# Dividing the last contraction, norm and stores at token 384 instead of 256

## The chip, the cores and the metric

One core of a Trainium2 chip. The metric is device microseconds of one execution. Engines are named as in the profile: PE is TensorE (matrix products; PEld its weight loads), DVE is VectorE, ACT is ScalarE, SP is SyncE, which issues nearly all DMAs. The program is written engine by engine, with semaphores between the engines; no scheduler moves anything.

## The reference

Two transformer blocks, 512 tokens, 1024 channels, float32. The change touches the end of the second one only: the down projection of its last MLP, the residual add, the final norm and the output.

```python
def rmsnorm(x, g):
    xf = x.astype(jnp.float32)
    y = xf * lax.rsqrt(jnp.mean(xf * xf, axis=-1, keepdims=True) + EPS) * g.astype(jnp.float32)
    return y.astype(x.dtype)

def sq_relu_mlp(h, w_up, w_down):
    u = jax.nn.relu(h @ w_up)
    return (u * u) @ w_down

def second_block(x, ..., ln_final):
...
        h = h + sq_relu_mlp(rmsnorm(h, ln_mlp[layer]), w_up[layer], w_down[layer])
    return rmsnorm(h, ln_final)
```

## The kernel before

Activations lie with channels on the 128 partitions and tokens along a row: `h` is 8 chunks of 128 channels by 512 tokens. A product with float32 accuracy is made of three (`exact3`): high weights by high data, low weights by high data, high weights by low data, where high and low are a rounded float32 kind (fp32r in the profile's rows) that TensorE takes in one pass. Each of the three loads its own 128 x 128 weights. A plain float32 product, as in the column sums, is one row of the program and two records in the trace.

The last MLP's down projection adds to `h` group by group. The very last of its work is kept apart, and is the stage that the change touches: output chunks 4 to 7 (`j` of 0 to 3), contracted over the last 8 groups of 128 hidden channels (`kt`), from the weight blocks `N_END - 2` and `N_END - 1`. So a chunk is 8 x 3 = 24 products. This stage is made in two parts of the tokens (`th` of 0 and 1), all four chunks for the first part, then all four for the second. Before, the parts are `HALF`: tokens 0 to 255 and 256 to 511.

For each part and chunk the work goes around the engines:

- PE, `last_chunk`: 24 products into one of two PSUM banks (X[2], X[3]); the third chunk waits for the residual add of the first to free its bank (`tl_h`), and so on.
- DVE, `last_resid`: adds the bank to `h` and ends in `tl_h`.
- ACT, `last_square`: squares the new chunk into a scratch tile.
- DVE, `last_add`: adds the squares to a running sum (the squares of chunks 0 to 3 are in it already).

After a part's four chunks comes its norm: PE's `last_norm` sums over partitions (a product with ones, plain float32), ACT's `last_rsqrt` makes rstd by Ln and Exp, DVE's `last_scale` multiplies each of the eight chunks of `h` by the weight and rstd, and SP stores each chunk when it is scaled (`h_final`), in the order of the chunks, one DMA of 128 rows each. The first part's norm is woven into the second part's products: in PE's order `last_norm(0)` stands behind the second part's first chunk, and in DVE's order `last_scale(0)`, all eight, stands behind the second part's first residual add. Each engine takes its instructions strictly in the order written.

Of the kernel before, what the change touches and what calls it, by code (L numbers as in the profile page):

```python
# [20 lines left out]
T = 512  # L21
# [209 lines left out]
def program(nc, A, out):  # L231
# [4 lines left out]
    with ctx:  # L236
# [205 lines left out]
        def wide(t):  # L442

            return t.rearrange("p k n -> p (k n)").rearrange("p (k n) -> p k n", k=4)
        HALF = (slice(0, T // 2), slice(T // 2, T))

        def copies(w):
            return w[:, :, 0:P].rearrange("p k (j n) -> p k j n", j=4)[:, :, :, 0:GLR]
# [879 lines left out]
        @block.sync  # L1328
        def _(sp):
            def raw_free(n):  # L1330

                if n >= 4 and n - 4 in FAST:
                    sp.wait_ge(S["st_mm"], 7 * FAST[n - 4] + PRODUCT_NO["P4"])
                elif n >= 4 and n - 4 in MLP_AT:
                    sp.wait_ge(S["acc_done"], DONE[n - 3])
                elif n >= 4:
                    sp.wait_ge(S["w_lo_ready"], STD_NO[n - 4] + 1)

            def load(n, src, cols=BW):

                raw_free(n)
                sp.dma_start(raw[:, n % 4, :, 0:cols], src).then_inc(w_arrived[n % 4], 16)

            def load_plain(first):
                _, count, w, col = next(x for x in plain if x[0] == first)
                cols = GLR if first == N_GLR else BW
                for j in range(count):
                    load(first + j, w[:, :, col + BW * j:col + BW * j + cols], cols)

            def load_wide_part(n, w, half, j):  # L1350
                raw_free(n + j)
                sp.dma_start(wide(raw[:, (n + j) % 4]),
                             w[:, 4 * half:4 * half + 4, 512 * j:512 * j + 512]).then_inc(w_arrived[(n + j) % 4], 16)

            def load_wide(n, w, half):
                for j in range(2):
                    load_wide_part(n, w, half, j)

            def load_mlp(n):
                up, down = mlps[n]  # L1360
                for i in range(32):
                    _, _, kind, g, b = MLP_AT[n + i]
                    if kind == "U":
                        load(n + i, up[:, :, 512 * g + BW * b:512 * g + BW * b + BW])
                    else:
                        raw_free(n + i)
                        sp.dma_start(wide(raw[:, (n + i) % 4]),
                                     down[:, 4 * g:4 * g + 4, 512 * b:512 * b + 512]).then_inc(w_arrived[(n + i) % 4], 16)

            _, _, first, col = next(x for x in plain if x[0] == N_DQ)  # L1370
            sp.dma_start(raw[:, 0, 0:4, :], first[:, 0:4, col:col + BW]).then_inc(S["ld_w0"], 16)
            sp.dma_start(vec[:], A["vecs"]).then_inc(S["ld_vec"], 16)
            for c in range(KT):
                if c == 2:
                    sp.dma_start(raw[:, 0, 4:8, :], first[:, 4:8, col:col + BW]).then_inc(w_arrived[0], 16)
                sp.dma_start(h[:, c, :], A["x"][:, c, :]).then_inc(S[f"ld_x{c}"], 16)
            load(N_DQ + 1, first[:, :, col + BW:col + 2 * BW])
            sp.dma_start(cst[:], A["consts"]).then_inc(S["ld_const"], 16)
            for n in (N_DK, N_DV, N_RW, N_RW + 1):
                load_plain(n)  # L1380
            for n in (N_MK, N_MV):
                load_plain(n)
            load_wide(N_WOA, mix_w, 1)
            sp.wait_ge(S["acc_done"], DONE[N_WOA])

            def reload(c):
                sp.dma_start(h[:, c, :], A["x"][:, c, :]).then_inc(S[f"ld_x{c}"], 16)

            for c in range(4):
                reload(c)  # L1390
            sp.wait_ge(S["acc_evac"], ACC[N_WOA] + 1)
            load_wide_part(N_WOB, mix_w, 0, 0)
            sp.wait_ge(S["acc_evac"], ACC[N_WOA] + 2)
            for c in range(4, KT):
                reload(c)
            sp.wait_ge(S["acc_evac"], ACC[N_WOA] + 4)
            load_wide_part(N_WOB, mix_w, 0, 1)
            sp.wait_ge(S["acc_evac"], ACC[N_WOA] + 5)
            load_plain(N_MQ)
            load_wide(N_MOA, mo_w, 0)  # L1400
            load_wide(N_MOB, mo_w, 1)
            load_mlp(N_MLP1)
            for n in (N_GLR, N_GQK, N_GV, N_GG, N_GOUT):
                load_plain(n)
            load_mlp(N_MLP2)
            for n in (N_KV, N_WQ):
                load_plain(n)
            load_wide(N_SOA, so_w, 0)
            load_wide(N_SOB, so_w, 1)
            load_mlp(N_MLP3)  # L1410
            for th in range(2):
                for c in range(KT):
                    sp.wait_ge(S["h_final"], KT * (th + 1) + c + 1)
                    sp.dma_start(out[:, c, HALF[th]], h[:, c, HALF[th]]).then_inc(S["st_out"], 16)
            sp.wait_ge(S["st_out"], 16 * 2 * KT)


# [75 lines left out]
        def _(pe):  # L1493
# [490 lines left out]
            def last_chunk(th, j):  # L1984
                c = j % 2
                if th == 0 and j == 0:
                    wait("st_ev", 2 * len(FAST))
                if 4 * th + j >= 2:
                    wait("tl_h", 4 * th + j - 1)
                ws = slice(j * P, j * P + P)  # L1990
                for kt in range(KT):
                    m = N_END - 2 + kt // 4
                    if th == 0 and j == 0 and kt % 4 == 0:
                        block_ready(m)
                    u_hi, u_lo = u_of(2, 12 + kt // 2)
                    last = exact3(X[2 + c][:, 0:T // 2], wide(hi_of(m))[:, kt % 4, ws], wide(lo_of(m))[:, kt % 4, ws],
                                  u_hi[:, kt % 2, HALF[th]], u_lo[:, kt % 2, HALF[th]], kt == 0, kt == KT - 1)
                last.then_inc(S["tl_done"], 1)

            def last_norm(th):  # L2000
                wait("tl_add", 4 * (th + 1))
                mm(X[th][:, 0:T // 2], C("ones"), nt[2][:, HALF[th]], start=True, stop=True).then_inc(S["tl_step"], 1)

            for th in range(2):
                for j in range(4):
# [7 lines left out]
        def _(act):  # L2013
# [352 lines left out]
            def last_square(th, j):  # L2366
                act.wait_ge(S["tl_h"], 4 * th + j + 1)
                if j < 2:
                    act.wait_ge(S["norm_add"], 7 * 7 + 3)
                else:  # L2370
                    act.wait_ge(S["tl_add"], 4 * th + j - 1)
                nc.scalar.activation(nt[j % 2][:, HALF[th]], h[:, 4 + j, HALF[th]], ACT.Square).then_inc(S["tl_sq"], 1)

            def last_rsqrt(th):
                act.wait_ge(S["tl_step"], 3 * th + 1)
                nc.scalar.activation(rstd[:, HALF[th]], X[th][:, 0:T // 2], ACT.Ln, scale=1.0 / D,
                                     bias=C("eps6")).then_inc(S["tl_step"], 1)
                act.wait_ge(S["tl_step"], 3 * th + 2)
                nc.scalar.activation(rstd[:, HALF[th]], rstd[:, HALF[th]], ACT.Exp, scale=-0.5).then_inc(S["tl_step"], 1)

            for th in range(2):
                for j in range(4):
# [7 lines left out]
        def _(dve):  # L2390
# [555 lines left out]

            def last_resid(th, j):
                dve.wait_ge(S["tl_done"], 4 * th + j + 1)
                h_ = h[:, 4 + j, HALF[th]]
                TTO(h_, h_, X[2 + j % 2][:, 0:T // 2], ALU.add).then_inc(S["tl_h"], 1)  # L2950

            def last_add(th, j):
                dve.wait_ge(S["tl_sq"], 4 * th + j + 1)
                if j:
                    dve.wait_ge(S["tl_add"], 4 * th + j)
                else:
                    dve.wait_ge(S["norm_add"], 7 * 7 + 3)
                TTO(nt[2][:, HALF[th]], nt[2][:, HALF[th]], nt[j % 2][:, HALF[th]], ALU.add).then_inc(S["tl_add"], 1)

            def last_scale(th):  # L2960
                dve.wait_ge(S["tl_step"], 3 * th + 3)
                for c in range(KT):
                    STT(h[:, c, HALF[th]], h[:, c, HALF[th]], V("ln_final_2", c), rstd[:, HALF[th]], ALU.mult,
                        ALU.mult).then_inc(S["h_final"], 1)

            for th in range(2):
                for j in range(4):
                    last_resid(th, j)
                    if j:
                        last_add(th, j - 1)  # L2970
                    elif th:
                        last_scale(0)
                last_add(th, 3)
            last_scale(1)


INPUTS = ["x", "mem", "norm_mix_w", "w_in", "mu_shift", "w_decay0", "w_decay_up", "a0", "a_up", "g_up", "k_k", "k_a", "r_k",
# [26 lines left out]
```

## Time and profile before

| | |
|---|---|
| time, median of 3 runs | 1936.69 us (1936.63 to 1937.65) |
| profiled execution, first to last instruction | 1937.4 us |
| mean granted TensorE clock | 0.998 |
| PE busy | 1912.2 us, 99% |
| DVE busy | 1333.0 us, 69% |
| ACT busy | 837.4 us, 43% |
| last stage's products, first to last | 1904.57 to 1928.20 us |
| after them, to the end of the span | 9.2 us |

The span is the time from the program's first to its last instruction in the one execution that was profiled; times in the trace are counted from its start. The page gives no other time for that execution. An instruction's record can be longer than the distance to the next of its kind, since both PE's products and its loads overlap: for a stream, the distance from start to start counts, and it is worked out from merged rows ("x8") as the row's length less one record, over the count less one.

### The profile page before, as it was taken

To read this page: it belongs to the slowest core of one execution; us is meant where nothing else is said; L and a number is where in the kernel's file an instruction comes from. 1 tells how busy PE (TensorE), PEld (TensorE's weight loads), DVE (VectorE), ACT (ScalarE), POOL (GpSimd) and SP (SyncE) were. 2 spreads that over 40 slices of the span, in tenths; PEclk is the share of its full clock that TensorE was granted. 3 is DMA by queue.
4 is the path that set the end of the run, shared out by engine and by line. 5 is a ranking of instruction groups with operands and counts; after the bars stand their busy time and mean duration, and the time that the engine had idled before them with its cause. 6 is when DMAs were issued, how large, how long until landed. Compare 5 with 4: busy or idle time off the path is not lost.

```text
span 1937.4 us, 32713 instructions
## 1 busy us (share of the span) xinstructions
PE 1912.2 (99%) x14002; PEld 1646.6 (85%) x14002; DVE 1333.0 (69%) x1755; ACT 837.4 (43%) x1254; POOL 121.1 (6%) x130
## 2 busy tenths in 40 slices
PE   8999999999999999999999999999999999999998
PEld 6877898888788898887989889889987788898897
DVE  5576869576677777767545687767677768777665
ACT  4333744344354344344224443434444645344342
POOL 1055100000000000010000000000002300000000
PEclk9999999999999999999999999999999999999999
DMA  8221402237123233224220233323342113233231
GB/s 271 88 66 66 137 10 80 88 132 128 46 89 108 87 110 109 88 78 140 90 87 23 66 98 98 109 87 109 102 144 88 50 47 106 90 106 109 87 109 44
DMA packets 138831, 182.62 MB, mean 94 GB/s; under 512 B 4917, under 2 KB 103429, under 8 KB 138304
## 3 DMA queue, kind: packets, MB, share of 16 engines
q1 hardware_dynamic: 135392, 168.91, 26.9%
q0 software_dynamic: 3296, 11.63, 2.9%
q8 instruction: 111, 1.82, 0.4%
q14 instruction: 32, 0.26, 0.0%
HBM read 172.66 MB, written 7.34 MB: 93 GB/s over the span
## 4 chain that ended last, share of the span: by engine, by line
PE 94%; DVE 3%; ACT 1%; issue 1%; DMA 0%; SPq 0%; DVEq 0%; ACTq 0%
PE X L1597 20%; PE M L1509 19%; PE M L1510 19%; PE M L1511 19%; PE X L643 3%; PE M L1570 1%; PE M L1571 1%; PE M L1572 1%; PE M L1925 1%; PE X L1902 1%; PE X L1913 1%; PE X L1780 1%; PE X L1749 1%; DMA raw<-in_w_in_dram 0%; PE X L1511 0%
## 5 line engine op out<-in xcount | busy, mean ns | idle before, releaser
L1510 PE MATMUL M<-u,raw_lo 128*128 128x512 f32 x728 | 287.9, 396 | 0.0
L1509 PE MATMUL M<-u,w_hi 128*128 128x512 f32 x728 | 287.9, 395 | 0.0
L1511 PE MATMUL M<-u,w_hi 128*128 128x512 f32 x728 | 286.1, 393 | 0.0
L2021 ACT ACTIVATE w_hi<-raw 128x2048 fp32r<-128x2048 f32 x113 | 215.6, 1908 | 93.5 <-PE M L1511 47.9
L2076 ACT ACTIVATE us<-X 128x256 f32<-128x256 f32 x156 | 60.2, 386 | 426.9 <-PE X L1597 426.9
L2549 DVE TENSOR_TENSOR h<-h,M 128x512 f32<-128x512 f32 x184 | 123.7, 685 | 144.7 <-PE M L1511 144.6
L1597 PE MATMUL X<-t,w_hi 128*128 128x256 f32 x936 | 173.2, 282 | 0.0
L1511 PEld LDWEIGHTS M<-u,w_hi 128*128 128x128 f32 x728 | 137.6, 189 | 32.8
L1509 PEld LDWEIGHTS M<-u,w_hi 128*128 128x128 f32 x728 | 136.8, 188 | 30.8
L1510 PEld LDWEIGHTS M<-u,raw_lo 128*128 128x128 f32 x728 | 136.7, 188 | 29.8
L2399 DVE TENSOR_TENSOR raw_lo<-raw,w_hi 128x2048 fp32r<-128x2048 f32 x57 | 130.3, 2287 | 23.7 <-ACT w_hi L2021 23.7
L1597 PEld LDWEIGHTS X<-t,w_hi 128*128 128x128 f32 x936 | 146.4, 188 | 0.0
L2399 DVE TENSOR_TENSOR w_lo<-raw,w_hi 128x2048 fp32r<-128x2048 f32 x52 | 118.9, 2289 | 29.9 <-ACT w_hi L2021 29.9
L1597 PE MATMUL X<-t,w_lo 128*128 128x256 f32 x468 | 131.7, 281 | 0.0
L1597 PE MATMUL X<-f,wx 128*128 128x256 f32 x624 | 117.8, 282 | 0.0
L1597 PEld LDWEIGHTS X<-f,wx 128*128 128x128 f32 x624 | 98.6, 189 | 1.7
L2480 DVE TENSOR_TENSOR w_lo<-w_sum,w_hi 128x1024 fp32r<-128x1024 f32 x78 | 91.9, 1220 | 0.0
L1597 PEld LDWEIGHTS X<-t,w_lo 128*128 128x128 f32 x468 | 88.2, 188 | 0.0
L1597 PE MATMUL X<-f,raw_lo 128*128 128x256 f32 x312 | 87.9, 282 | 0.0
L1509 PE MATMUL M<-gx_hi,w_hi 128*128 128x512 f32 (+2 forms) x232 | 85.1, 367 | 1.0 <-DVE w_lo L2399 0.5
L1511 PE MATMUL M<-gx_lo,w_hi 128*128 128x512 f32 (+2 forms) x232 | 84.3, 363 | 0.0
L1510 PE MATMUL M<-gx_hi,w_lo 128*128 128x512 f32 (+2 forms) x232 | 84.3, 363 | 0.0
(525 smaller groups left out, 4542.2 us busy)
## 6 DMA issues: line engine op xcount, KB each, us to landing
raw<-in_w_up_dram SPq DMA_DIRECT2D x48, 1024.0 KB, 5.4
raw<-in_w_down_dram SPq DMA_DIRECT2D x48, 1024.0 KB, 5.0
raw<-in_w_in_dram SPq DMA_DIRECT2D x12, 1024.0 KB, 8.6
raw<-in_a_w_in_dram SPq DMA_DIRECT2D x12, 1024.0 KB, 5.3
h<-in_x_dram SPq DMA_DIRECT2D x16, 256.0 KB, 4.8
raw<-in_w_mk_dram SPq DMA_DIRECT2D x4, 1024.0 KB, 4.9
raw<-in_w_mv_dram SPq DMA_DIRECT2D x4, 1024.0 KB, 5.2
raw<-in_w_out_dram SPq DMA_DIRECT2D x4, 1024.0 KB, 5.1
```

The source lines that it names most:

```text
L643: last = mm(blk(bank, hh, cp, cpar), a_, b_, start=True, stop=True)
L1509: mm(dst, wh, xh, start=start, stop=False)
L1510: mm(dst, wl, xh, start=False, stop=False)
L1511: return mm(dst, wh, xl, start=False, stop=stop)
L1570: mm(o_, hi[:, kt, ts_], w_hi[:, n % 2, kt, cs], start=kt == 0, stop=False)
L1571: mm(o_, hi[:, kt, ts_], w_lo[:, n % 2, kt, cs], start=False, stop=False)
L1597: last = mm(region(r), (wl if p_ == 1 else wh)[:, m, :], xl if p_ == 2 else xh, start=name in ("P1", "P2", "P4", "P5") and m == 0 and p_ = ...
L2021: nc.scalar.activation(hi_of(n)[:, :, :], raw[:, n % 4], ACT.Copy).then_inc(S["w_hi_ready"], 1)
L2076: nc.scalar.activation(at_, region(r), ACT.Copy).then_inc(S["st_snap"], 1)
L2399: TTO(lo_of(n)[:, :, :], raw[:, n % 4], hi_of(n)[:, :, :].bitcast(f32), ALU.subtract).then_inc(S["w_lo_ready"], 1)
L2480: TTO(to_, from_, hi_.bitcast(f32), ALU.subtract).then_inc(S["st_lo"], 1)
L2549: TTO(h[:, 4 * b + c, :], h[:, 4 * b + c, :], acc(n + i, c), ALU.add).then_inc(S["acc_evac"], 1)
```

## The change

Both parts keep their work, and their border moves from token 256 to token 384: the first part has 384 tokens, the second 128. Every instruction of the stage has the same count as before, at the new width. DVE's scaling of the first part is cut in two groups of four chunks: chunks 0 to 3 behind the second part's second residual add and first sum, chunks 4 to 7 behind the second part's last sum.

```diff
         HALF = (slice(0, T // 2), slice(T // 2, T))
+        LAST, LAST_AT = (3 * T // 4, T // 4), (slice(0, 3 * T // 4), slice(3 * T // 4, T))
...
                     sp.wait_ge(S["h_final"], KT * (th + 1) + c + 1)
-                    sp.dma_start(out[:, c, HALF[th]], h[:, c, HALF[th]]).then_inc(S["st_out"], 16)
+                    sp.dma_start(out[:, c, LAST_AT[th]], h[:, c, LAST_AT[th]]).then_inc(S["st_out"], 16)
...
-                    last = exact3(X[2 + c][:, 0:T // 2], wide(hi_of(m))[:, kt % 4, ws], wide(lo_of(m))[:, kt % 4, ws],
-                                  u_hi[:, kt % 2, HALF[th]], u_lo[:, kt % 2, HALF[th]], kt == 0, kt == KT - 1)
+                    last = exact3(X[2 + c][:, 0:LAST[th]], wide(hi_of(m))[:, kt % 4, ws], wide(lo_of(m))[:, kt % 4, ws],
+                                  u_hi[:, kt % 2, LAST_AT[th]], u_lo[:, kt % 2, LAST_AT[th]], kt == 0, kt == KT - 1)
...
-                mm(X[th][:, 0:T // 2], C("ones"), nt[2][:, HALF[th]], start=True, stop=True).then_inc(S["tl_step"], 1)
+                mm(X[th][:, 0:LAST[th]], C("ones"), nt[2][:, LAST_AT[th]], start=True, stop=True).then_inc(S["tl_step"], 1)
...
-            def last_scale(th):
+            def last_scale(th, c0, c1):
                 dve.wait_ge(S["tl_step"], 3 * th + 3)
-                for c in range(KT):
-                    STT(h[:, c, HALF[th]], h[:, c, HALF[th]], V("ln_final_2", c), rstd[:, HALF[th]], ALU.mult,
+                for c in range(c0, c1):
+                    STT(h[:, c, LAST_AT[th]], h[:, c, LAST_AT[th]], V("ln_final_2", c), rstd[:, LAST_AT[th]], ALU.mult,
                         ALU.mult).then_inc(S["h_final"], 1)
...
                     last_resid(th, j)
                     if j:
                         last_add(th, j - 1)
-                    elif th:
-                        last_scale(0)
+                    if th and j == 1:
+                        last_scale(0, 0, 4)
                 last_add(th, 3)
-            last_scale(1)
+            last_scale(0, 4, KT)
+            last_scale(1, 0, KT)
```

`last_square`, `last_rsqrt`, `last_resid` and `last_add` have the same replacement of `HALF` and `T // 2`.

DVE's order from the second part's first residual add to the end; `h` is the residual, `nt` the sum and the squares, `vec` the norm weights. Before:

```order
L2950 TENSOR_TENSOR h<-h,X 128x256
L2963 SCALAR_TENSOR_TENSOR h<-h,vec,rstd 128x256 x8
L2950 TENSOR_TENSOR h<-h,X 128x256
L2958 TENSOR_TENSOR nt_64<-nt_64,nt_62 128x256
L2950 TENSOR_TENSOR h<-h,X 128x256
L2958 TENSOR_TENSOR nt_64<-nt_64,nt_63 128x256
L2950 TENSOR_TENSOR h<-h,X 128x256
L2958 TENSOR_TENSOR nt_64<-nt_64,nt_62 128x256
L2958 TENSOR_TENSOR nt_64<-nt_64,nt_63 128x256
L2963 SCALAR_TENSOR_TENSOR h<-h,vec,rstd 128x256 x8
```

And now, with every line number one higher:

```order
L2951 TENSOR_TENSOR h<-h,X 128x128 x2
L2959 TENSOR_TENSOR nt_64<-nt_64,nt_62 128x128
L2964 SCALAR_TENSOR_TENSOR h<-h,vec,rstd 128x384 x4
L2951 TENSOR_TENSOR h<-h,X 128x128
L2959 TENSOR_TENSOR nt_64<-nt_64,nt_63 128x128
L2951 TENSOR_TENSOR h<-h,X 128x128
L2959 TENSOR_TENSOR nt_64<-nt_64,nt_62 128x128
L2959 TENSOR_TENSOR nt_64<-nt_64,nt_63 128x128
L2964 SCALAR_TENSOR_TENSOR h<-h,vec,rstd 128x384 x4
L2964 SCALAR_TENSOR_TENSOR h<-h,vec,rstd 128x128 x8
```

Four scalings of the first part moved from ahead of the second residual add to behind the first sum, and four from there to behind the last sum.

PE's order where the first part's column sum stands between the second part's first chunk and its second; `u` and `ux` are the data in high (0) and low (1), `w_hi` and `raw_lo` the weights, `cst` the ones. Before:

```order
L1510 MATMUL X<-ux_0_176,raw_lo 128x256
L1511 MATMUL X<-ux_1_177,w_hi 128x256
L2002 MATMUL X<-nt_64,cst 128x256
L1509 MATMUL X<-u_0_174,w_hi 128x256
L1510 MATMUL X<-u_0_174,raw_lo 128x256
```

And now:

```order
L1511 MATMUL X<-ux_0_176,raw_lo 128x128
L1512 MATMUL X<-ux_1_177,w_hi 128x128
L2003 MATMUL X<-nt_64,cst 128x384
L1510 MATMUL X<-u_0_174,w_hi 128x128
L1511 MATMUL X<-u_0_174,raw_lo 128x128
```

Nothing moved here: the column sum is wider, the products of the second part around it are narrower, and there are as many as before.

## Rows read from the trace of the kernel before

**Rows 1.** The page: span, busy time, and the chain that ended last.

```profile
span 1937.4 us, 32713 instructions
PE 1912.2 (99%) x14002; PEld 1646.6 (85%) x14002; DVE 1333.0 (69%) x1755; ACT 837.4 (43%) x1254; POOL 121.1 (6%) x130
...
PE 94%; DVE 3%; ACT 1%; issue 1%; DMA 0%; SPq 0%; DVEq 0%; ACTq 0%
```

**Rows 2.** The chain that ended last, from 1893 us: start, length, what.

```profile
1893.57 0.24 PE M L1509
...
1904.73 0.12 PE X L1509
...
1928.24 0.43 DVE h L2950
1928.69 0.42 ACT nt L2372
1929.14 0.44 DVE nt L2958
1929.62 0.71 PE X L2002 x2
1930.36 0.48 ACT rstd L2376
...
1931.31 0.48 DVE h L2963
```

**Rows 3.** DVE's timeline in the last stage: start, length, instruction, idle time before.

```profile
1907.65 0.42 DVE L2950 TENSOR_TENSOR h<-h,X 128x256 f32<-128x256 f32 x1 [0.74 <-PE X L1511]
...
1916.29 0.42 DVE L2950 TENSOR_TENSOR h<-h,X 128x256 f32<-128x256 f32 x1 [2.12 <-PE X L1511]
...
1931.31 3.25 DVE L2963 SCALAR_TENSOR_TENSOR h<-h,vec,rstd 128x256 f32<-128x256 f32 x8 [1.75 <-ACT rstd L2379]
```

**Rows 4.** PE's timeline around the first part's column sum (L2002).

```profile
1918.85 0.28 PE L1511 MATMUL X<-ux,w_hi 128*128 128x256 f32 x1
1918.97 0.60 PE L2002 MATMUL X<-nt,cst 128*128 128x256 f32 x2
...
1919.52 0.29 PE L1510 MATMUL X<-u,raw_lo 128*128 128x256 f32 x1
```

**Rows 5.** PE's and PEld's timelines elsewhere: one-column and 128-column products, plain f32.

```profile
29.16 0.95 PE L1582 MATMUL X<-cst,nt 128*128 128x1 f32 x8
...
29.16 0.86 PEld L1582 LDWEIGHTS X<-cst,nt 128*128 128x128 f32 x7 [0.24 <-issue]
...
1015.83 1.95 PE L1051 MATMUL M<-gat,gv 128*128 128x128 f32 x16
```

**Rows 6.** Weight loads by line and form: busy us, mean ns of one, idle before.

```profile
L1511 PEld LDWEIGHTS M<-gx_lo,w_hi 128*112 128x112 f32 x8 | 1.4, 174 | 0.5
...
L1511 PEld LDWEIGHTS X<-u,w_hi 128*128 128x128 f32 x48 | 9.1, 189 | 0.0
...
L1015 PEld LDWEIGHTS X<-gq,gk 128*64 128x64 f32 x32 | 2.2, 137 | 0.5
```

**Rows 7.** SP's DMAs: ns min/median/max, first and last start; and merged.

```profile
L1414 SPq DMA_DIRECT2D out_dram<-h x8: 332/450/453, 1931.8 to 1935.1; - x8
...
DMA to landing us min/median/max: 1.7/1.8/1.9
...
1931.82 3.77 SPq L1414 DMA_DIRECT2D out_dram<-h  x8
...
L1387 SPq DMA_DIRECT2D h<-in_x_dram x8: 327/432/434, 305.1 to 326.1; - x8
```

**Rows 8.** DVE by line and form, other widths: busy us, mean ns of one.

```profile
L2498 DVE SCALAR_TENSOR_TENSOR us<-us,rstd 128x512 f32<-128x512 f32 x39 | 27.0, 693 | 1.3
...
L2700 DVE TENSOR_REDUCE small<-X 128x1 f32<-128x384 f32 x8 | 4.1, 553 | 0.1
...
L2700 DVE TENSOR_REDUCE small<-X 128x1 f32<-128x128 f32 x8 | 2.0, 286 | 0.1
```

More of the change, by code:

```diff
@@ L2371, in last_square @@
                     act.wait_ge(S["tl_add"], 4 * th + j - 1)
-                nc.scalar.activation(nt[j % 2][:, HALF[th]], h[:, 4 + j, HALF[th]], ACT.Square).then_inc(S["tl_sq"], 1)
+                nc.scalar.activation(nt[j % 2][:, LAST_AT[th]], h[:, 4 + j, LAST_AT[th]], ACT.Square).then_inc(S["tl_sq"], 1)
             def last_rsqrt(th):
                 act.wait_ge(S["tl_step"], 3 * th + 1)
-                nc.scalar.activation(rstd[:, HALF[th]], X[th][:, 0:T // 2], ACT.Ln, scale=1.0 / D,
+                nc.scalar.activation(rstd[:, LAST_AT[th]], X[th][:, 0:LAST[th]], ACT.Ln, scale=1.0 / D,
                                      bias=C("eps6")).then_inc(S["tl_step"], 1)
                 act.wait_ge(S["tl_step"], 3 * th + 2)
-                nc.scalar.activation(rstd[:, HALF[th]], rstd[:, HALF[th]], ACT.Exp, scale=-0.5).then_inc(S["tl_step"], 1)
+                nc.scalar.activation(rstd[:, LAST_AT[th]], rstd[:, LAST_AT[th]], ACT.Exp, scale=-0.5).then_inc(S["tl_step"], 1)
             for th in range(2):
@@ L2948, in last_resid @@
                 dve.wait_ge(S["tl_done"], 4 * th + j + 1)
-                h_ = h[:, 4 + j, HALF[th]]
-                TTO(h_, h_, X[2 + j % 2][:, 0:T // 2], ALU.add).then_inc(S["tl_h"], 1)
+                h_ = h[:, 4 + j, LAST_AT[th]]
+                TTO(h_, h_, X[2 + j % 2][:, 0:LAST[th]], ALU.add).then_inc(S["tl_h"], 1)
             def last_add(th, j):
@@ L2957, in last_add @@
                     dve.wait_ge(S["norm_add"], 7 * 7 + 3)
-                TTO(nt[2][:, HALF[th]], nt[2][:, HALF[th]], nt[j % 2][:, HALF[th]], ALU.add).then_inc(S["tl_add"], 1)
-            def last_scale(th):
+                TTO(nt[2][:, LAST_AT[th]], nt[2][:, LAST_AT[th]], nt[j % 2][:, LAST_AT[th]], ALU.add).then_inc(S["tl_add"], 1)
+            def last_scale(th, c0, c1):
                 dve.wait_ge(S["tl_step"], 3 * th + 3)
-                for c in range(KT):
-                    STT(h[:, c, HALF[th]], h[:, c, HALF[th]], V("ln_final_2", c), rstd[:, HALF[th]], ALU.mult,
+                for c in range(c0, c1):
+                    STT(h[:, c, LAST_AT[th]], h[:, c, LAST_AT[th]], V("ln_final_2", c), rstd[:, LAST_AT[th]], ALU.mult,
                         ALU.mult).then_inc(S["h_final"], 1)
```

## The prediction

> **What bounds the kernel now.** The page comes first: TensorE is busy for 1912.2 us of a span of 1937.4 us and carries 94% of the chain that ended last [rows 1]. Up to the end the kernel is therefore a stream of products on one engine, and only two things can move its time: the rate of that stream, and what runs after its last product. The change touches nothing before the last stage, so the second view is the end of the chain [rows 2]. There the reader is to see three stretches. First the stream: 48 products of 512 columns from 1893.57 to 1904.73, which is 0.2325 us from one to the next, then 192 products of 256 columns. Then a ladder of single steps across VectorE, ScalarE and TensorE, each waiting for the one before: residual, square, sum, column sum over partitions, Ln, Exp, from 1928.24 to 1931.31, 3.07 us. Then the scaling and the stores.
>
> The third view is VectorE's timeline in the last stage [rows 3]. Its residual adds mark the ends of the output chunks: the first at 1907.65, the fourth at 1916.29, so 2.88 us for a chunk of 24 products, 0.120 us each. The PE never waits there. The fourth view is SyncE's queue [rows 7]: the last eight stores begin between 1931.8 and 1935.1, (3.77 - 0.45)/7 = 0.47 us apart, while VectorE delivers one scaled chunk every (3.25 - 0.48)/7 = 0.40 us [rows 3]. So in the tail it is not the scaling that sets the end but the issue of the stores: the last one starts 6.9 us after the last residual add begins, and lands 1.8 us later.
>
> **The change, part by part.** It keeps the number of every instruction: 96 products and 96 weight loads for either part, eight scalings and eight stores for either part. What changes is the width, 256 and 256 tokens to 384 and 128, and the place of four scalings. I count from the first product of the stage, and call D the start of the last residual add (1928.24 now).
>
> *First part, 96 products of 384 columns.* None of this kind and width is in the rows. They lie between 0.120 us at 256 and 0.2325 at 512 [rows 2, 3]; the middle is 0.176. If the time were proportional to columns, 512 would give 0.174 and 256 would give 0.180, and these are my bounds. 96 x (0.176 - 0.120) = +5.4 us, bounds +5.2 and +5.8.
>
> *Second part, 96 products of 128 columns.* This is the disputed price. By the same straight line (0.1125 us for 256 more columns) 128 columns would take 0.064 us, and the second part would give back exactly what the first costs. But each product has its own weight load of 128 columns, since high and low weights alternate. What such a load costs when the product beside it does not hide it is seen where the products are a single column wide: eight of them take 0.95 us, and their loads begin (0.86 - 0.19)/6 = 0.112 us apart [rows 5]. A one-column product has nothing to stream, so 0.112 us is the load. Products of 128 columns in plain f32 come at the same distance, (1.95 - 0.28)/15 = 0.112 us for 16 of them [rows 5]. Those weights are plain f32 and the ones of this stage are the rounded kind, so I compare the load records: in the rounded kind a load of 112 columns lasts 174 ns and one of 128 lasts 189 [rows 6], about 0.9 ns a column, which is 0.11 us for 128; a load of 64 columns lasts 137 and fits the same slope. The loads begin 0.120 us apart now, hidden by products of 0.120; behind products of 128 columns they stand in the open. I take 0.112. Bounds: 0.120 above while loads are all that counts (nothing saved), 0.064 below if loads overlap one another; and above everything 0.224, two f32 records of 0.112, if narrow products of the rounded kind were run as plain f32 ones are, which take two records each. 96 x (0.112 - 0.120) = -0.8 us.
>
> The Trainium skill speaks against this step (TensorE: Matmul & The Clock Gate, section "Back-to-back issue gap"): it gives a sustained 81 ns for a load and a product of 128 columns, and 131 ns at 512. The trace does not agree at 512, where this stream takes 232 ns; at 128 no row here has this kind of product. With 81 ns the second part would give 96 x (0.081 - 0.120) = -3.7 us and the sum below would end at +1.9 us, 1938.6 us.
>
> *The first part's column sum.* It stands in TensorE's queue behind the second part's first chunk, and delays the next chunk: the product expected at 1919.09 (0.12 after 1918.97) starts at 1919.52, so 0.43 us [rows 4]. With 384 in place of 256 columns that is 0.65: +0.2 us.
>
> So D moves by +5.4 - 0.8 + 0.2 = +4.8 us.
>
> *The moved scalings.* The first four (384 wide) now stand on VectorE behind the second residual add and the first sum of the second part. A 256-wide scaling comes every 0.40 us; from 256 to 512 the record grows from 0.48 to 0.69 [rows 2, 8], so 384 wide costs about 0.10 more, 0.50 us, and 128 wide 0.29. Behind the four (2.0 us) waits the third residual add. They can start when chunk 1 is finished and its add and sum are done, and chunk 2 takes 24 x 0.112 = 2.7 us, so they are covered with about 0.1 us to spare. Were that cover gone, the third residual would be late, which no product waits for: chunks 2 and 3 only need the first two. Cost nothing. ScalarE's wider squares and rsqrt steps of the first part lie beside 2.7 us chunks and cost nothing either.
>
> *The tail.* The remaining four wide scalings stand between the last sum and the narrow scalings. After D: residual and square take 0.45 each now with their handovers [rows 2]; VectorE's records fall from 553 ns at 384 to 286 at 128 [rows 8], 0.13 per 128 columns, so 0.32 and 0.33 now, and the sum 0.29 instead of 0.42. The first wide scaling starts at D + 0.94 and is finished at D + 1.53, the fourth at D + 3.03. The ladder to the second rstd, 3.07 us before, would be about 2.2, but VectorE is occupied until D + 2.95. From then on it delivers a narrow chunk every 0.29 us, faster than SyncE takes them. SyncE's issue does not depend on the bytes: 450 ns for stores of 1 KB per partition, 432 for loads of 2 KB [rows 7]. The fourth wide store starts at D + 3.06, eight narrow ones follow 0.47 apart, the last at D + 6.85. Before it was D + 6.9. So the shorter ladder and the narrower scaling are real and buy nothing: twelve stores now queue behind D where eight did. I take 0; bounds -1.6 us (if issue fell to VectorE's 0.29 a narrow store, last start D + 5.3) and +0.5 (one store more in the way).
>
> **Sum.** +4.8 us on the profiled span of 1937.4, and the same on the median of the three runs, 1936.69, which lies 0.7 lower: **1941.5 us**. About 0.2% (3.9 us) can be told from no change, so this is slower by a little more than that. With the bounds of this case (+5.2 - 0.8 + 0.2 - 1.6 = +3.0, and +5.8 + 0 + 0.2 + 0.5 = +6.5) it is 1939.7 to 1943.2.
>
> **The rivals.**
>
> 1. *Narrow products cost what they stream.* Loads overlap one another and 128 columns take 0.064 us. For it: the load record is 0.19 us long and already overlaps the next one, begun 0.12 later. Against it: one-column products at 0.112 [rows 5]. Then D moves by +5.4 - 5.4 + 0.2, and the time is 1936.9 us: no change, because the tail is held by the stores. This rival decides, ending at "same", once a narrow product takes less than 0.102 us: (5.4 + 0.2 - 3.9)/96 = 0.018 below 0.120.
>
> 2. *Narrow products of this kind run like plain f32, two passes.* For it: every product of this kind in the rows is 256 or 512 wide, so nothing shows a narrow one at the fast rate. Against it: at 256 columns this kind takes 0.120 us where a plain f32 product takes 0.43 [rows 4], and the change alters nothing in an instruction but its width. Then 96 x (0.224 - 0.120) = +10.0, and with +5.4 and +0.2 the time is 1952.3 us, 0.8% slower.
>
> 3. *The tail does shrink.* The narrow stores are issued as fast as VectorE delivers, -1.6 us: 1939.9 us, which counts as no change. For it: the first issue after a pause lasted 332 ns and not 450 [rows 7]. Against it: loads of twice the bytes issue no slower.
>
> 4. *The change does what it is built for*, narrow products at streaming price and a tail shorter by 1.6 us: 1935.3. Even that is no change by 0.2%; to be faster by 3.9 us it would need something that I see nowhere.
>
> **How the numbers follow.** Load-bound narrow products with the tail held by SyncE: 72%. Rival 3 under the same price: 6%. Rival 1, with prices in between: 8%. Rival 2: 10%. Rival 4 and what I don't see: 4%. Slower by over 0.2% is most of the first (69 of 72, since its lower edge lies under the bound), rival 2 and a little of the rest: 0.80. Same: 0.18. Faster: 0.02. The range reaches down to rival 1 and leaves out rival 2: 1936.8 to 1943.2, some 84%.
>
> **What would show it.** In the changed kernel's profile: weight loads of the second part 0.11 us apart and 24 products in 2.7 us, products idle between them; the first part's residual adds 4.2 us apart; D near 1933; twelve stores back to back from 1.6 us after D, the last starting 6.9 us after D; the narrow scalings waiting for VectorE and not for Exp. The prediction is wrong if the second part's chunks take 1.5 us (rival 1) or 5.3 us (rival 2), or if SyncE's stores stand less than 0.4 us apart.

## The result, and the profile after

The changed kernel takes 1941.56 us (median of 11 runs, 1939.36 to 1943.62) against 1936.69 of the kernel before (11 runs): the ratio is 1.0026, with a 95% interval of 1.0018 to 1.0033, or 3.5 to 6.4 us. It is slower, by 4.9 us where 4.8 were forecast.

The page of the changed kernel shows the same picture as before at its head:

```profile
span 1940.3 us, 32713 instructions
PE 1915.7 (99%) x14002; PEld 1651.0 (85%) x14002; DVE 1332.6 (69%) x1755; ACT 837.4 (43%) x1254; POOL 120.8 (6%) x130
```

The two spans can't simply be subtracted. The last stage's first product starts at 1904.57 us in the profile of before and at 1903.02 in this one, though nothing ahead of it was changed; in the seven experiments below it lies between 1900.29 and 1903.39. So I compare two stretches that don't contain this wandering: the *stage*, from the last stage's first product to the start of the last residual add, and the *tail*, from there to the end of the span. VectorE's timeline of the changed kernel, which answers to [rows 3]:

```profile
1907.45 0.56 DVE L2951 TENSOR_TENSOR h<-h,X 128x384 f32<-128x384 f32 x1 [2.09 <-PE X L1512]
1911.68 0.56 DVE L2951 TENSOR_TENSOR h<-h,X 128x384 f32<-128x384 f32 x1 [3.67 <-PE X L1512]
...
1922.76 0.29 DVE L2951 TENSOR_TENSOR h<-h,X 128x128 f32<-128x128 f32 x1 [0.93 <-PE X L1512]
1926.08 0.29 DVE L2951 TENSOR_TENSOR h<-h,X 128x128 f32<-128x128 f32 x1 [3.04 <-PE X L1512]
...
1926.49 2.20 DVE L2964 SCALAR_TENSOR_TENSOR h<-h,vec,rstd 128x384 f32<-128x384 f32 x4
1928.76 0.29 DVE L2951 TENSOR_TENSOR h<-h,X 128x128 f32<-128x128 f32 x1
...
1931.44 0.29 DVE L2951 TENSOR_TENSOR h<-h,X 128x128 f32<-128x128 f32 x1 [2.19 <-PE X L1512]
...
1932.31 4.30 DVE L2964 SCALAR_TENSOR_TENSOR h<-h,vec,rstd 128x384 f32<-128x384 f32 x12
```

(The last row merges twelve scalings, four of 384 columns and eight of 128.) Read the distances of the adds: 4.23 us between the first part's chunks and 2.68 between the second part's last three, where a chunk of before took 2.88 [rows 3]. From the second part's first add to its second, 3.32: the first part's column sum stands between them. The stage has grown from 1928.24 - 1904.57 = 23.67 us to 1931.44 - 1903.02 = 28.42, and the tail has shrunk from 9.14 to 8.88.

PE's and PEld's timelines: the first product of each part, then the second part around the column sum and behind it, against [rows 4, 5]:

```profile
1903.02 0.35 PE L1510 MATMUL X<-u,w_hi 128*128 128x384 f32 x1
...
1919.93 0.22 PE L1510 MATMUL X<-u,w_hi 128*128 128x128 f32 x1
...
1922.55 0.86 PE L2003 MATMUL X<-nt,cst 128*128 128x384 f32 x2
...
1923.31 0.28 PE L1511 MATMUL X<-u,raw_lo 128*128 128x128 f32 x1
1923.42 0.28 PE L1512 MATMUL X<-u,w_hi 128*128 128x128 f32 x1
1923.54 0.27 PE L1510 MATMUL X<-u,w_hi 128*128 128x128 f32 x1
1923.65 0.27 PE L1511 MATMUL X<-u,raw_lo 128*128 128x128 f32 x1
```

```profile
1923.47 0.19 PEld L1510 LDWEIGHTS X<-u,w_hi 128*128 128x128 f32 x1
1923.59 0.19 PEld L1511 LDWEIGHTS X<-u,raw_lo 128*128 128x128 f32 x1
1923.70 0.19 PEld L1512 LDWEIGHTS X<-u,w_hi 128*128 128x128 f32 x1
```

A product every 0.11 us, at the loads' own pace, as the one-column products of [rows 5] came. One sign that the prediction named can't be seen: a product's record lasts 0.28 us and reaches over the next, so PE counts as busy for 11.47 of the second part's 11.51 us and no idle time shows between the products. SyncE's stores behind the last residual add, against [rows 7] (ns min/median/max, first and last start):

```profile
L1415 SPq DMA_DIRECT2D out_dram<-h x12: 332/430/454, 1933.0 to 1938.3; - x12
...
DMA to landing us min/median/max: 1.6/1.7/2.0
```

There are twelve, the last 1938.3 - 1931.4 = 6.9 us behind the add, as before. It lands a little sooner, 1.6 us after its start for 1.8.

### The profile page after: what moved, and what is told of

The parts are those of the page before. It is cut to its first block, busy times and chain, and to the rows that moved or that the text cites. A ratio compares the mean times of both kernels' runs of the same rounds, so it can differ in the third digit from the quotient of the medians.

```text
span 1940.3 us, 32713 instructions
## 1 busy us (share of the span) xinstructions
PE 1915.7 (99%) x14002; PEld 1651.0 (85%) x14002; DVE 1332.6 (69%) x1755; ACT 837.4 (43%) x1254; POOL 120.8 (6%) x130
## 4 chain that ended last, share of the span: by engine, by line
PE 94%; DVE 3%; ACT 1%; issue 1%; DMA 0%; SPq 0%; DVEq 0%; ACTq 0%
PE X L1598 20%; PE M L1510 19%; PE M L1511 19%; PE M L1512 19%; PE X L644 3%; PE M L1571 1%; PE M L1573 1%; PE M L1572 1%; PE M L1926 1%; PE X L1903 1%; PE X L1914 1%; PE X L1781 1%; PE X L1750 1%; PE X L1512 0%; PE X L1511 0%
## 5 line engine op out<-in xcount | busy, mean ns | idle before, releaser
L1510 PEld LDWEIGHTS M<-u,w_hi 128*128 128x128 f32 x728 | 136.8, 188 | 30.8
```

What stands on the lines that cost most here:

```text
L1510: mm(dst, wh, xh, start=start, stop=False)
```

## The experiments

e1 to e5 are edits of the changed kernel, e6 and e7 of the kernel before. Each ratio stands against runs of the kernel before that were made beside it, with medians of 1936.69 us for the changed kernel, 1936.41 for e1 to e4 and 1936.32 for e5 to e7; it is estimated from all runs and need not be the quotient of two medians. Stage and tail are read from each run's profile, as above.

| kernel | time, us | ratio to before (95%) | stage, us | tail, us |
|---|---|---|---|---|
| before | 1936.69 | | 23.67 | 9.14 |
| changed, 384/128, two groups | 1941.56 | 1.0026 (1.0018 to 1.0033) | 28.42 | 8.88 |
| e1: 320/192, two groups | 1937.64 | 1.0008 (0.9999 to 1.0017) | 25.52 | 9.00 |
| e2: 448/64, two groups | 1946.65 | 1.0053 (1.0041 to 1.0066) | 34.70 | 8.85 |
| e3: 256/256, two groups | 1936.75 | 0.9999 (0.9990 to 1.0008) | 23.67 | 9.26 |
| e4: 384/128, one group | 1942.06 | 1.0029 (1.0018 to 1.0041) | 29.12 | 7.92 |
| e5: changed, stores by two engines | 1939.95 | 1.0019 (1.0010 to 1.0028) | 28.42 | 8.00 |
| e6: before, stores by two engines | 1935.95 | 0.9999 (0.9990 to 1.0008) | 23.67 | 9.08 |
| e7: before, GpSimd scales three of eight | 1936.73 | 1.0004 (0.9995 to 1.0013) | 23.67 | 9.74 |

The first two ask why a narrow product costs 0.112 us. My theory is its weight load; the rival is that the rounded kind streams at half the rate when it is narrower than 256 columns, which gives the same number at 128.

**e1, the border at 320.**

```diff
-        LAST, LAST_AT = (3 * T // 4, T // 4), (slice(0, 3 * T // 4), slice(3 * T // 4, T))
+        LAST, LAST_AT = (320, T - 320), (slice(0, 320), slice(320, T))
```

> The changed kernel with the border at token 320: parts of 320 and 192 tokens. Load theory: a product of under about 240 columns costs its weight load, 0.112 us, so 192 columns cost what 128 did; 320 columns cost 0.148 us by the straight line. Products 96 x (0.148 + 0.112) = 25.0 us, and with the first part's column sum (0.54) and 0.2 of handover the last residual add starts 25.7 us after the stage's first product (23.7 before, 28.4 changed): the time is 2.0 us over before, 1938.7. Width theory: products of the rounded kind that are narrower than 256 columns stream at half the rate, as a plain f32 record does (0.43 us for 512 columns), which gives the same 0.11 us at 128 columns but 0.165 at 192: 96 x (0.148 + 0.165) = 30.0 us, the add starts 30.8 us after the first product, and the time is 7 us over before, 1943.8.

Measured: PE's timeline in the second part, now 192 columns wide, shows the same distance of 0.11 us as at 128:

```profile
1921.57 0.28 PE L1512 MATMUL X<-u,w_hi 128*128 128x192 f32 x1
1921.68 0.27 PE L1510 MATMUL X<-u,w_hi 128*128 128x192 f32 x1
1921.79 0.28 PE L1511 MATMUL X<-u,raw_lo 128*128 128x192 f32 x1
1921.90 0.28 PE L1512 MATMUL X<-u,w_hi 128*128 128x192 f32 x1
```

The stage takes 25.52 us (25.7 by the load theory, 30.8 by the width theory). Half the width more changed nothing in the price, so it isn't width that sets it. The time is 1937.64 against the 1936.41 of before, 1.2 us more; the 2.0 expected lie inside its interval of -0.2 to 3.3 us.

**e2, the border at 448.**

```diff
-        LAST, LAST_AT = (3 * T // 4, T // 4), (slice(0, 3 * T // 4), slice(3 * T // 4, T))
+        LAST, LAST_AT = (448, T - 448), (slice(0, 448), slice(448, T))
```

> The changed kernel with the border at token 448: parts of 448 and 64 tokens. Load theory: 64 columns still cost 0.112 us, and 448 cost 0.204: 96 x 0.316 = 30.3 us, and with 0.75 for the column sum and 0.2 the last residual add starts 31.3 us after the stage's first product; the time is 7.6 us over before, 1944.3. Width theory (half rate under 256 columns): 64 columns cost 0.06 us, 96 x 0.264 = 25.3, the add starts 26.3 us after the first product, the time is 2.6 us over before, 1939.3. So the two theories order this run and the one at 320 the opposite way. The tail stays: twelve stores behind the last residual add, the last starting some 7 us after it.

Measured: the load theory again, but with a surprise on top. The stage takes 34.70 us, above the 31.3 expected. For most of the second part 64 columns cost 0.11 us, as 192 and 128 do. Then the distance doubles:

```profile
1928.84 0.28 PE L1512 MATMUL X<-u,w_hi 128*128 128x64 f32 x1
1928.95 0.28 PE L1510 MATMUL X<-u,w_hi 128*128 128x64 f32 x1
1929.07 0.34 PE L1511 MATMUL X<-u,raw_lo 128*128 128x64 f32 x1
...
1929.44 0.40 PE L1510 MATMUL X<-u,w_hi 128*128 128x64 f32 x1
1929.65 0.40 PE L1511 MATMUL X<-u,raw_lo 128*128 128x64 f32 x1
1929.86 0.40 PE L1512 MATMUL X<-u,w_hi 128*128 128x64 f32 x1
```

and the table by stretches shows why (busy us and count of PE, PEld, DVE, ACT, POOL, then the granted clock, DMA share, GB/s):

```profile
1921.79:1927.80 6.01, 6.01 (x51) 5.64 (x50) 2.00 (x4) 2.04 (x4) 0.00 (x0) 1.00 0.02 4
1927.80:1931.50 3.70, 3.70 (x25) 3.70 (x24) 2.74 (x6) 0.26 (x1) 0.00 (x0) 0.68 0.50 185
1931.50:1936.70 5.20, 5.16 (x25) 5.03 (x24) 0.36 (x2) 0.26 (x1) 0.00 (x0) 0.50 0.12 45
```

TensorE's clock fell from full to half, 2.4 to 1.2 GHz, while loads and 64-column products were following each other without a pause; its busy share in the table stayed full. At the lower level a load with its product costs 0.214 us instead of 0.112. The products at that distance, from 1929.22 on, are 34: 34 x 0.10 = 3.4 us, which is the excess over 31.3. It was not this execution alone: the mean granted clock is 0.995 or 0.996 in all five timed runs of e2, and 0.998 or 0.999 in those of e1 and of the changed kernel. What made the clock fall stays open: the changed kernel's second part has the same loads beside 128-column products for 11.5 us, at 1.00. In that kernel the granted clock is 1.00 from the stage's first product to the last residual add, so this has no part in its time.

The next two take the change apart.

**e3, the groups without the new border.**

```diff
-        LAST, LAST_AT = (3 * T // 4, T // 4), (slice(0, 3 * T // 4), slice(3 * T // 4, T))
+        LAST, LAST_AT = (256, T - 256), (slice(0, 256), slice(256, T))
```

> The changed kernel with the border back at token 256: of the change only the scaling in two groups is left. Store-queue theory: VectorE has four more scalings behind the last sum (4 x 0.40 = 1.6 us), which end before Exp does, and SyncE has twelve stores behind the last residual add instead of eight. The first of them can start 1.8 us after that add, the twelfth 11 x 0.47 later, at 7.0 us; before, the last store started at 6.9. Time within 0.3 us of before, 1936.7. If the scalings in the tail were what costs time (rival), the end would come 1.6 us later, 1938.3.

Measured: no change in time, and the last store starts at 7.0 us behind the add, as the queue of twelve at 0.47 us gives:

```profile
L1415 SPq DMA_DIRECT2D out_dram<-h x12: 332/448/453, 1925.7 to 1931.0; - x12
```

The add starts at 1923.96, so 1931.0 is 7.0 behind it. Four scalings were put into the tail and the tail grew by 0.12 us: their 1.6 us lie beside the ladder to rstd. (This run and the next move scalings and stores together; e5 moves the issue of stores alone.)

**e4, the new border without the groups.**

```diff
-                    if th and j == 1:
-                        last_scale(0, 0, 4)
+                    elif th:
+                        last_scale(0, 0, KT)
                 last_add(th, 3)
-            last_scale(0, 4, KT)
             last_scale(1, 0, KT)
```

> The changed kernel with the border at 384, but the first part's eight scalings in one group behind the second part's first residual add, as before. Store-queue theory: all eight stores of the first part are issued while products still run, so only eight narrow stores stand behind the last residual add. VectorE's eight wide scalings take 4.2 us there and delay the second residual add, for which chunk 3's products wait: the last add starts about 0.5 us later after the stage's first product than in the changed kernel (28.9 for 28.4). Then the ladder to the second rstd is short (2.3 us) and uncovered, the first narrow store starts 2.65 us after the add and the last at 6.0 for 6.85. Sum: 0.4 us less than the changed kernel, 1941.1. If the issue of stores did not hold the tail, its last store would start no earlier than in the changed kernel and the time would be 0.5 us more, 1942.1.

Measured: the stage is 0.70 us longer than the changed kernel's (0.5 expected), since the second residual add now stands behind eight wide scalings and chunk 3's products wait for it:

```profile
1924.33 4.33 DVE L2964 SCALAR_TENSOR_TENSOR h<-h,vec,rstd 128x384 f32<-128x384 f32 x8 [1.58 <-ACT rstd L2380]
1928.57 0.28 DVE L2951 TENSOR_TENSOR h<-h,X 128x128 f32<-128x128 f32 x1
...
1928.91 0.33 PE L1510 MATMUL X<-u,w_hi 128*128 128x128 f32 x1 [0.48 <-DVE h L2951]
...
1931.84 0.29 DVE L2951 TENSOR_TENSOR h<-h,X 128x128 f32<-128x128 f32 x1 [2.32 <-PE X L1512]
```

The tail is 0.96 shorter, with eight stores between 1934.5 and 1937.7 behind an add at 1931.84. By the two stretches that is 0.26 us less than the changed kernel. The times, 1942.06 and 1941.56 beside different runs of before, with ratios of 1.0029 and 1.0026, can't tell so little. It shows what the groups are worth at this border: they keep the products flowing and pay for it in the store queue, about even.

The last three ask whether the tail can be made shorter once it is known to hang on the stores.

**e5, four of the second part's stores issued by ScalarE.**

```diff
-                for c in range(KT):
+                for c in range(0, KT, 1 + th):
                     sp.wait_ge(S["h_final"], KT * (th + 1) + c + 1)
...
             last_rsqrt(1)
+            for c in range(1, KT, 2):
+                act.wait_ge(S["h_final"], 2 * KT + c + 1)
+                act.dma_start(out[:, c, LAST_AT[1]], h[:, c, LAST_AT[1]]).then_inc(S["st_out"], 16)
```

> The changed kernel, with four of the second part's eight stores (chunks 1, 3, 5, 7) issued by ScalarE, which has nothing left to do, and the others by SyncE as before. Store-queue theory: issue no longer limits, and the last store starts when the last narrow scaling is done, 5.2 us after the last residual add instead of 6.85: 1.6 us less than the changed kernel, 1939.9. If the DMA engines or the bytes held the tail (rival), the stores would be issued earlier but land later, and the span would end as far behind the last residual add as in the changed kernel (8.9 us).

Measured: half of each. The last store starts 5.3 us behind the add, 1.5 sooner than in the changed kernel, but the tail ends only 0.88 us sooner, because this store takes 2.3 us to land instead of 1.6. The issues, and below them how busy the 16 DMA engines were in 40 slices from 1931.0 us to the end (tenths, GB/s):

```profile
L1415 SPq DMA_DIRECT2D out_dram<-h x8: 332/388/464, 1931.0 to 1934.5; - x8
L2390 ACTq DMA_DIRECT2D out_dram<-h x4: 338/342/374, 1933.2 to 1934.9; - x4
...
DMA to landing us min/median/max: 1.7/1.8/2.3
```

```profile
DMA  0000059999999999999999999999985000000000
GB/s 0 0 0 0 0 188 366 366 329 367 376 357 395 329 413 320 376 357 320 279 276 276 273 282 276 285 276 257 288 248 148 13 19 19 0 0 0 0 0 0
```

The engines are 90% busy or more until the last store: behind the issue stands the next limit. That the time, 1939.95, is the 1939.9 expected is luck: 3.6 us over before, with an interval of 1.9 to 5.4, it can't tell 0.88 from 1.6.

**e6, the same for the kernel before.** The edit is that of e5, with `HALF[1]` in place of `LAST_AT[1]`.

> The kernel before, border at 256, with the same four of the second part's stores issued by ScalarE. Store-queue theory: the last store starts when the last scaling is done, 6.35 us after the last residual add instead of 6.9: about 0.5 us less than before, 1936.2, which the times alone can hardly tell. If the DMA engines held the tail, nothing would change behind the add (9.2 us to the span's end).

Measured: the queue theory where the last store starts, the rival where it ends. It starts at 6.37 us behind the add for 6.91 before, the expected half microsecond, and lands 2.3 us later for 1.8: the tail is 9.08 for 9.14, so that the end stays where it was. In the profile of before, slices between the last eight stores fall to 125 to 250 GB/s again and again (40 slices from 1931.5 us to the end):

```profile
DMA  0000000189679849949956984994896698100000
GB/s 0 0 0 0 0 0 0 42 299 347 195 250 354 257 146 347 326 153 319 333 181 222 354 278 160 354 319 125 305 333 209 229 347 292 35 0 0 0 0 0
```

Now, in 40 slices from 1928.6 us to the end, they stay full:

```profile
DMA  0000000299589999999999999999960000000000
GB/s 0 0 0 0 0 0 0 92 353 318 184 297 367 332 325 339 339 325 360 339 339 325 346 339 361 318 311 318 332 233 28 28 21 21 0 0 0 0 0 0
```

The Trainium skill (DMA: Bandwidth & Descriptors, section "Issuing engines are not separate DMA queues") has it that DMAs issued from several engines run on the same 16 DMA engines. The trace agrees: of the 0.54 us by which the last store started sooner, 0.06 is left at the end of the span.

**e7, three of the second part's scalings on GpSimd, kernel before.**

ScalarE's prescaling stands ahead of the second part's squares, GpSimd's products at the end of its program, and the stores at the end of ScalarE's; VectorE scales and SyncE stores only chunks 3 to 7 of the second part.

```diff
+                if th:
+                    for c in range(3):
+                        nc.scalar.activation(h[:, c, HALF[1]], h[:, c, HALF[1]], ACT.Copy, scale=V("ln_final_2", c))
...
+            pool.wait_ge(S["tl_step"], 6)
+            for c in range(3):
+                nc.gpsimd.tensor_tensor(h[:, c, HALF[1]], h[:, c, HALF[1]], rstd[:, HALF[1]], ALU.mult).then_inc(S["sw_p"], 1)
...
+            for c in range(3):
+                act.wait_ge(S["sw_p"], KT + c + 1)
+                act.dma_start(out[:, c, HALF[1]], h[:, c, HALF[1]]).then_inc(S["st_out"], 16)
```

> The kernel before, border at 256, with three of the second part's eight scalings taken off VectorE: ScalarE multiplies chunks 0 to 2 by the norm weights ahead of the last norm, GpSimd multiplies them by rstd behind it, and ScalarE issues their stores. If the tail's length is VectorE's scaling and SyncE's issue together, both of which lose three of eight: five scalings and five stores behind rstd, the last store starting about 5.4 us after the last residual add instead of 6.9, so 1.5 us less than before, 1935.2. GpSimd's 128 x 256 product took 0.61 us elsewhere, three of them 1.9, about as long as VectorE's five. If GpSimd and VectorE slow each other down when they work on the same buffers (rival), the gain is under 0.5 us.

Measured: the rival, and a second cost on top. The last store starts 6.75 us behind the add, 0.16 sooner than before where 1.5 were expected. In the groups of instructions of the tail, both engines' records have grown (count, busy us, mean ns); the third row is GpSimd's product of that shape elsewhere in the kernel before:

```profile
L2974 DVE SCALAR_TENSOR_TENSOR h<-h,vec,rstd 128x256 f32<-128x256 f32 x5 | 3.6, 774 | 1.8 <-ACT rstd L2383 1.8
L1492 POOL TENSOR_TENSOR h<-h,rstd 128x256 f32<-128x256 f32 x3 | 2.4, 842 | 380.8 <-ACT rstd L2383 380.8
...
L1486 POOL TENSOR_TENSOR sc<-sc,small 128x256 f32<-128x256 f32 x8 | 4.9, 609 | 54.8 <-DVE small L2891 54.8
```

VectorE's five scalings take 3.56 us from first to last, more than its eight took alone (3.25, [rows 3]). Those that ran beside GpSimd's three, which ended at 1929.97, and those that came after (ns min/median/max, first and last start):

```profile
L2974 DVE SCALAR_TENSOR_TENSOR h<-h,vec,rstd x3: 939/941/1046, 1927.5 to 1929.3; 128x256 f32<-128x256 f32 x3
...
L2974 DVE SCALAR_TENSOR_TENSOR h<-h,vec,rstd x2: 471/472/473, 1930.2 to 1930.6; 128x256 f32<-128x256 f32 x2
```

The Trainium skill has this (SBUF — State Buffer, section "Who interferes with whom"): a VectorE instruction with two inputs in SBUF contends with a GpSimd instruction that reads SBUF. The trace agrees: 0.94 to 1.05 us beside GpSimd, 0.47 without it.

The tail is 0.6 us longer all the same, and that is not the stores: the last one lands 8.6 us behind the add, where it was 8.7. What ends later is GpSimd's program. At its end stands a DRAIN, which begins as its three products do and lasts 6.4 us, until 1933.9; the span ends at 1934.1. In the kernel before the same instruction lasts 7.3 us, but it begins at 1547.3 and is long done:

```profile
L236 POOLq DRAIN x1: 6415/6415/6415, 1927.5 to 1927.5; - x1
...
L236 POOLq DRAIN x1: 7292/7292/7292, 1547.3 to 1547.3; - x1
```

No version tried is measurably faster than the kernel before.

## Why the prediction was right

**The widest term, the first part:** 96 products of 384 columns take 1919.93 - 1903.02 = 16.91 us, 0.176 each, the middle of the straight line, for 11.52 before: +5.4 as forecast. The 320 and 448 columns of e1 and e2 lie on the same line: their first parts' adds stand 3.52 and 4.90 us apart, which is 0.147 and 0.204 us a product.

**The disputed term, the second part:** 2.68 us a chunk, 0.112 us a product; 4 x (2.68 - 2.88) = -0.8, as forecast. The rows that it was forecast from are records, two to a plain float32 product, and not products, as the prediction calls them; rival 2 counts them rightly. That the price is the load's and not the width's is shown by e1 and e2: it is the same at 192, 128 and, at full clock, 64 columns. So rival 1 (0.064) and rival 2 (0.224) are both out, and the 81 ns of the Trainium skill (TensorE: Matmul & The Clock Gate, section "Back-to-back issue gap") do not hold for this kind of product with a load of its own: the trace has 112.

A third reading, that any two products stand at least 0.112 us apart whatever they load, was not tested by a run, but rows of the kernel before speak against it. Where the load has 64 columns (plain float32), loads begin (0.54 - 0.14)/7 = 0.057 us apart and the 64-column products (0.68 - 0.22)/7 = 0.066:

```profile
1018.60 0.68 PE L1015 MATMUL X<-gq,gk 128*64 128x64 f32 x8
1018.60 0.54 PEld L1015 LDWEIGHTS X<-gq,gk 128*64 128x64 f32 x8
```

**The column sum:** 3.32 - 2.68 = 0.64 us for 0.43: +0.2, as forecast.

**The moved scalings** were covered, but only just. They took 0.53 us each and not 0.50, 2.20 us for the four, and the third residual add follows them at once, with no idle time ahead of it in its row. No product waited: the distance of the adds stayed 2.68.

**The tail** was sized right to its store, 6.85 us behind the add, and the mechanism held: four scalings and four stores more in the tail cost 0.12 us in e3, four of each fewer give back 0.96 in e4, and in e5, where only the issue changes, the last store starts 1.5 us sooner. For the kernel before, that the issue sets the end is too simple: in e6 the issue is relieved, the DMA engines are then nine tenths busy, and the end stays where it was. What I had taken as 0 is -0.26, mostly because a store of 64 KB lands in 1.6 us where one of 128 KB took 1.8. Rival 3, a faster issue of small stores, is out: 430 ns for a store of 64 KB, 450 for one of 128. Rival 4, which needs rivals 1 and 3 together, goes with them.

The terms add up to +4.75 - 0.26 = +4.5 us by the two profiles, and the times give +4.9, with an interval of 3.5 to 6.4. That the terms came out is no luck; that the sum agrees with the time to 0.1 us is. The last residual add, which the prediction put near 1933, starts at 1931.44, because the stage itself starts 1.55 us sooner in this execution.

One thing in the prediction's background was wrong without harm. I put the profiled span of 1937.4 beside the median of 1936.69 as if they were the same measure. In the timed runs of the changed kernel, and in the 49 of the kernel before that stand beside the experiments, the time is 1.8 us above the span. So the profiled execution of before took some 1939.2 us, more than any of its timed runs; the sum, a difference, did not depend on it.

## What to carry to other kernels

By the prices of this case, dividing a stream of products unevenly is free only while every piece is wide enough to hide its weight load. Find the load's price where products of one column, or narrow ones, show it in the open (here 0.112 us), and the width that hides it on the line of the wide products (here some 240 columns, an estimate from 0.120 us at 256 and 0.2325 at 512), and count narrower pieces at the load's price. Before shortening the work in a tail, look at which queue ends it: here the scaling and the norm became shorter and the end did not come sooner, since the number of stores behind the last step had grown from eight to twelve. Once the issue of stores is relieved, look at the DMA engines as the next limit (e5, e6). And before giving late work to an engine that had finished, look at how its program ends: GpSimd's DRAIN, unseen before, came to hold the end of the span (e7).

## What the runs showed of the hardware that I had not expected

- TensorE's clock fell to half while it was busy without a pause, in a stretch of 64-column products each with its own load (e2, granted clock 1.00, then 0.50 from 1929.1 us on). With 128 and 192 columns it stayed at 1.00 to the end of the stage. A load with its product slows with the clock, from 0.112 to 0.214 us.
- Two engines issuing stores brought the DMA engines to nine tenths busy, at 297 to 367 GB/s in all slices of the stores but one, and the last landing from 1.8 to 2.3 us (e6).
- GpSimd and VectorE, multiplying at the same time from SBUF, took 0.84 and 0.77 us a 128 x 256 instruction on the mean (e7), where GpSimd took 0.61 elsewhere in the kernel before and VectorE 0.48 alone. VectorE's were back at 0.47 once GpSimd had finished.
- GpSimd's DRAIN at the end of its program lasted 6.4 to 7.3 us. It cost nothing where GpSimd had finished early, and 0.6 us of tail where its last work stood in the tail (e7).
